# A two-layer hybrid encoder on one core: attention's values by batches of three positions, and FFN inner tiles in two chunks of 11

## The reference

```python
for i in range(DEPTH):
    h_res = h_res + 0.5 * swiglu(rms_norm(h_res, ffn1_norm[i]), ffn1_w_in[i], ffn1_w_out[i])
    h = rms_norm(h_res, mix_norm[i])
    proj = h @ w_in[i]
    y_a = conv_module(proj[..., :o_conv], ...)          # GLU, causal depthwise conv of 31 taps, LayerNorm, swish
    q, k, v = ...                                       # 16 query heads, 4 key/value heads of 64, RMS-normed q and k
    y_b = window_sink_attention(q, k, v, attn_sinks[i]) @ attn_w_out[i]
    merged = gates[..., :D_MODEL] * y_a + gates[..., D_MODEL:] * y_b
    h_res = h_res + merged @ w_out[i]
    h_res = h_res + 0.5 * swiglu(rms_norm(h_res, ffn2_norm[i]), ffn2_w_in[i], ffn2_w_out[i])
```

## Time and profile before

| | us |
|---|---|
| runs | 2418.34, 2423.99, 2425.91 (median 2423.99) |
| profiled execution, its own time | 2424.94 |
| its span | 2423.1 |
| PE busy | 2378.2 (98%), 17637 instructions |
| DVE busy | 1720.2 (71%) |
| ACT busy | 1222.0 (50%) |
| POOL busy | 345.3 (14%) |
| granted TensorE clock, mean | 0.992 |

### The profile page before, as it was taken

One profiled execution on the slowest core, in us unless ns is written; L12 is line 12 of the kernel. 1 busy time (PEld: TensorE's weight loads), 2 busy tenths in 40 slices (PEclk: granted clock), 3 DMA queues, 4 the chain that ended last, 5 costly groups with the idle time before them and its releaser, 6 DMA issues.

```text
span 2423.1 us, 43031 instructions
## 1 busy us (share of the span) xinstructions
PE 2378.2 (98%) x17637; PEld 2236.9 (92%) x17637; DVE 1720.2 (71%) x2740; ACT 1222.0 (50%) x1991; POOL 345.3 (14%) x454
## 2 busy tenths in 40 slices
PE   7999999999999999999999999999999999999999
PEld 6999999999999999999989999998888777889897
DVE  8766664798886477667787676647888855867584
ACT  7554543443444375546565455543434454746371
POOL 1010101121112210101001101011211122101010
PEclk9999999999999999999999999999999999999999
DMA  6655646666667966556546556466676698657472
GB/s 172 154 136 147 154 111 140 145 146 144 139 141 172 209 134 152 145 144 155 146 106 161 141 145 151 112 146 145 145 153 144 130 217 191 144 143 175 116 176 92
DMA packets 106756, 358.69 MB, mean 148 GB/s; under 512 B 12096, under 2 KB 12096, under 8 KB 106560
## 3 DMA queue, kind: packets, MB, share of 16 engines
q0 software_dynamic: 64080, 210.53, 43.0%
q1 hardware_dynamic: 42112, 145.08, 19.8%
q10 hardware_dynamic: 368, 0.33, 0.0%
HBM read 351.41 MB, written 2.10 MB: 146 GB/s over the span
## 4 chain that ended last, share of the span: by engine, by line
PE 87%; DVE 4%; DMA 4%; ACT 3%; issue 2%; POOL 0%; DVEq 0%; ACTq 0%; SPq 0%
PE po L1061 30%; PE po L1078 20%; PE po L1127 19%; PE ptr L1078 8%; PE pov L1078 5%; DMA wla<-in_mixes 1%; PE pov L1289 1%; PE pov L1287 1%; PE ptr L1268 1%; PE pstat L1252 1%; DMA raw<-in_pairs 1%; PE pov L1224 1%; DVE rms L1520 0%; PE pstat L1227 0%; DMA wha<-in_mixes 0%
## 5 line engine op out<-in xcount | busy, mean ns | idle before, releaser
L1061 PE MATMUL po<-xh,wha 128*128 128x264 f32 (+1 forms) x1408 | 348.2, 314 | 4.5 <-DMA wla<-in_mixes 3.9
L1061 PE MATMUL po<-xl,wha 128*128 128x264 f32 (+1 forms) x1408 | 339.2, 308 | 0.0
L1061 PE MATMUL po<-xh,wla 128*128 128x264 f32 (+1 forms) x1408 | 338.4, 307 | 0.0
L1670 DVE SCALAR_TENSOR_TENSOR cv<-ub,lp,cv 128x528 f32<-128x528 f32 (+1 forms) x480 | 333.3, 754 | 1.7
L1061 PEld LDWEIGHTS po<-xh,wha 128*128 128x128 f32 x1408 | 230.3, 191 | 23.3 <-DVE t L1873 3.5
L1078 PE MATMUL po<-x7h,wha 128*128 128x264 f32 (+1 forms) x844 | 241.1, 286 | 4.1 <-ACT tmp L702 1.6
L1078 PE MATMUL po<-x7l,wha 128*128 128x264 f32 (+1 forms) x844 | 240.3, 285 | 0.0
L1061 PEld LDWEIGHTS po<-xh,wla 128*128 128x128 f32 x1408 | 229.7, 191 | 11.3
L1078 PE MATMUL po<-x7h,wla 128*128 128x264 f32 (+1 forms) x844 | 239.8, 284 | 0.0
L1061 PEld LDWEIGHTS po<-xl,wha 128*128 128x128 f32 x1408 | 229.7, 191 | 10.3
L658 ACT ACTIVATE wla<-wha 128x1024 fp32r<-128x1024 f32 x136 | 143.1, 1054 | 162.2 <-DMA wha<-in_mixes 162.1
(11 more groups left out here) (247 smaller groups left out, 6297.0 us busy)
## 6 DMA issues: line engine op xcount, KB each, us to landing
wha<-in_mixes POOLq DMA_DIRECT2D x136, 512.0 KB, 4.4
wla<-in_mixes POOLq DMA_DIRECT2D x136, 512.0 KB, 6.4
raw<-in_pairs SPq DMA_DIRECT2D x88, 768.0 KB, 5.1
wlb<-in_pairs POOLq DMA_DIRECT2D x45, 512.0 KB, 7.6
raw<-in_pairs SPq DMA_DIRECT2D x88, 256.0 KB, 5.9
wla<-in_pairs POOLq DMA_DIRECT2D x87, 256.0 KB, 6.7
wfa<-in_outs SPq DMA_DIRECT2D x48, 448.0 KB, 3.4
wla<-in_pairs POOLq DMA_DIRECT2D x41, 512.0 KB, 8.2
```

The costliest lines, as they stand in the source:

```text
L1061: ins = mm(po[:, 2 * out_slot + h, 0:width], w[:, k, :], v[:, k, t:t + width], start=begin and k == 0 and p == 0, stop=last and k == kt - ...
L1670: stt(cv[:, j, a:], u, w, cv[:, j, a:], ALU.mult, ALU.add).then_inc(conv_step, 1)
```

## The change

1. The attention's values are made for the three positions of a batch at once. `turn` and `take_pt` of single positions become, for a batch, `turn_later` (the windows of its second and third position, four transposes, which fill the bank `ptr`), `take_windows`, `turn_first` (the first position's windows and one transpose of all meta probabilities of the batch), `take_metas` and `mix_values`.
2. To have one transpose of the meta probabilities, `norm_p` writes them to a tile of their own, `pm` (96 columns), in an instruction of its own, and the windows in another; it waits for the meta transpose of the batch before.
3. The meta product of a position is two products, one for each half of the array's columns, with 96 rows: the weights `vz` are zero in the rows of the other positions. `head_stats` makes the meta values three times, at the partitions of the three positions, by six products with the identity, and `head_std` copies six pieces.
4. The steps stand at other places among the blocks of `mixer_in` and `attn_out_start`, and in ACT's order.
5. The inner tiles of an FFN run in two chunks of 11. A row of output products has two blocks of weights, of 6 and of 5 k-tiles, so that a chunk has 16 blocks (`NB`) for 8 rows. The ring of three remains, its buffers in another order. `out_hi` and `out_lo` serve two blocks a row.
6. `hh` and `hl` hold 11 tiles for 8, and the memory set aside for POOL's transfers is set to 4096 (`dynamic_dma_scratch_size`).

```diff
-CHUNKS = ((0, 7), (7, 14), (14, KF))
+CHUNKS = ((0, 11), (11, KF))
+CHUNK_T = 11
+
+BLOCKS = ((0, 6), (6, CHUNK_T))
+NB = KD * len(BLOCKS)
...
-OUT_UNITS = ((0, 2, 4), (8, 10, 12))
+OUT_UNITS = ((2, 4, 0), (10, 12, 8))
...
-    return USED["out", s, c, {"A": 6, "S12": 7, "S43": 5}[part]]
+    return USED["out", s, c, {"A": NB - 2, "S12": NB - 1, "S43": NB - 3}[part]]
...
-    return USED[("P2", "P6", "P7")[m], s * KF + CHUNKS[c][1] - 2]
+    return USED[("P6", "P7", "P2")[m], s * KF + CHUNKS[c][1] - 2]
...
-    return USED["out", 2 * l, len(CHUNKS) - 1, n + 4]
+    return USED["out", 2 * l, len(CHUNKS) - 1, NB - 4 + n]
...
                     for m in range(KD):
                         if m:
-                            out_hi(s, c, m + 2)
+                            out_hi(s, c, 2 * m + 2)
+                        out_hi(s, c, 2 * m + 3)
...
-            def take_pt(l, g, pos):
...
+            def take_windows(l, g, b):
+
+                act.wait_ge(tr_ready, 2 * batch(l, g, b) + 1)
+                act.wait_ge(pv_done, batch(l, g, b) + 1)
+                func(pt[:, 1:, :, :], ptr[:, :].rearrange("p (i h n) -> p i h n", i=2, h=2), ACT.Copy)\
+                    .then_inc(pt_ready, 1)
+
+            def take_metas(l, g, b):
+
+                act.wait_ge(tr_ready, 2 * batch(l, g, b) + 2)
+                if b:
+                    func(pt[:, 0, :, :], ptr[:, 0:2 * P].rearrange("p (h n) -> p h n", h=2), ACT.Copy)
+                n = MR - metas_from(l, b) * MB
+                func(ptm[0:n, :], ptr[0:n, 2 * P:3 * P], ACT.Copy).then_inc(pt_ready, 1)
...
-                    take_pt(l, g, 0)
+                    take_windows(l, g, 0)
                     fill_tanh(l, g, 7)
-                    attn_exp(l, g, 1, 0)
-                    take_pt(l, g, 1)
-                    attn_exp(l, g, 1, 1)
-                    attn_exp(l, g, 1, 2)
+                    for i in range(SB):
+                        attn_exp(l, g, 1, i)
                     h(8)
-                    take_pt(l, g, 2)
+                    take_metas(l, g, 0)
...
-                tr(pov[0:META, 64:64 + HD], kvp[HD:P, PAD:PAD + META], ident[HD:P, HD:P])
-                tr(pov[0:MB, 128:128 + HD], kvp[HD:P, PAD + META - MB:PAD + META], ident[HD:P, HD:P])\
-                    .then_inc(qk_stat, 1)
+                for c, t in ((64, PAD), (128, PAD + META - MB)):
+                    for i in range(SB):
+                        ins = mm(pov[i * MB:(i + 1) * MB, c:c + HD], kvp[HD:P, t:t + MB], ident[HD:P, HD:P], start=True,
+                                 stop=True)
+                ins.then_inc(qk_stat, 1)
...
+            def mix_values(l, g, b):
+
+                pe.wait_ge(pt_ready, 2 * batch(l, g, b) + 3)
+                pe.wait_ge(o_lo, batch(l, g, b) + 1)
...
+                    if pos:
+                        for h in range(2):
+                            mm(dst[h * HD:(h + 1) * HD], vw[:, pos - 1, :], cut(pt[:, i, h, :]), start=True,
+                               stop=False, skip_group_check=True)
                     for h in range(2):
-                        mm(dst[h * HD:(h + 1) * HD], vw[:, pos - 1, :], cut(pt[:, h, :]), start=True,
-                           stop=False, skip_group_check=True)
-                mm(dst, vm[:, :], cut(ptm[:, :]), start=pos == 0, stop=True,
-                   skip_group_check=True).then_inc(pv_done, 1)
+                        ins = mm(dst[h * HD:(h + 1) * HD], vz[0:n, i - i0, h, :], cut(ptm[0:n, :]), start=pos == 0,
+                                 stop=True, skip_group_check=True)
+                ins.then_inc(pv_done, 1)
...
-                    mids = {7: do(lambda: S(1)), 8: do(lambda: V(0), lambda: T(1)),
-                            9: do(lambda: V(2), lambda: T(3)), 10: do(lambda: V(4), lambda: T(5))}
-                    ends = {3: do(lambda: head_stats(l, g)), 5: do(lambda: S(0)), 7: do(lambda: T(0)),
-                            8: do(lambda: V(1), lambda: T(2), lambda: S(2)),
-                            9: do(lambda: V(3), lambda: T(4)), 10: do(lambda: V(5), lambda: T(6))}
+                    mids = {7: do(lambda: S(1)), 8: do(lambda: F(0)), 9: do(lambda: L(1)), 10: do(lambda: V(1))}
+                    ends = {3: do(lambda: head_stats(l, g)), 5: do(lambda: S(0)), 7: do(lambda: L(0)),
+                            8: do(lambda: V(0), lambda: S(2)), 9: do(lambda: F(1)), 10: do(lambda: L(2))}
...
-                            out_lo(s, c, m + 2)
+                            out_lo(s, c, 2 * m + 2)
+                        out_lo(s, c, 2 * m + 3)
...
+                dve.wait_ge(tr_ready, 2 * batch(l, g, b))
+                tt(pm[:, :].rearrange("p (i h k) -> p i h k", i=SB, h=2)[:, i0:, :, :],
+                   w[:, i0:, WIN:WIN + MB].rearrange("p i (h k) -> p i h k", h=2),
+                   rd.to_broadcast([P, SB - i0, 2, META]), ALU.mult)
...
-    nc = bacc.Bacc("TRN2", target_bir_lowering=False, num_devices=1)
+    nc = bacc.Bacc("TRN2", target_bir_lowering=False, num_devices=1, dynamic_dma_scratch_size=4096)
```

More of the change, by code:

```diff
@@ L502, in lead, with batch, metas_from @@
             return 1 if l == LAST else 0
-        def place(l, g, pos):
-            if l == LAST:
-                return l * GROUPS * NPOS + g * (NPOS - 1) + pos - 1
-            return (l * GROUPS + g) * NPOS + pos
+        def batch(l, g, b):
+            return (l * GROUPS + g) * NBAT + b
+        def metas_from(l, b):
+            return max(lead(l) - b * SB, 0)
         def o_from(l, b):
@@ L895, in take_o @@
             def take_o(l, g, b):
-                act.wait_ge(pv_done, place(l, g, (b + 1) * SB) + 1)
+                act.wait_ge(pv_done, batch(l, g, b) + 2)
                 dst, src = o_view(ah[:, 2 * g:2 * g + 2, :], l, b)
@@ L1255, in scores, with turn_windows @@
                 ins.then_inc(s_ready, 1)
-            def turn(l, g, pos):
-                if pos < lead(l):
-                    return
-                n = place(l, g, pos)
-                b, i = pos // SB, pos % SB
-                pe.wait_ge(p_ready, (l * GROUPS + g) * NBAT + b + 1)
-                pe.wait_ge(pt_ready, n + 1)
-                if pos:
+            def turn_windows(l, g, b, positions):
+                for n, i in enumerate(positions):
                     for h in range(2):
@@ L1901, in laid_out @@
             for a, b in CHUNKS:
-                outs += [block(f"{name}_w_out", l, a, b - a, ((m * P, P),)) for m in range(KD)]
+                for m in range(KD):
+                    outs += [block(f"{name}_w_out", l, a + k, z - k, ((m * P, P),)) for k, z in BLOCKS]
         for n in range(NBLK):
```

177 lines of the change are left out of this document (89 added, 88 removed).

## The result

| | us |
|---|---|
| runs after | 2387.31, 2391.09, 2391.75, 2393.29 (median 2391.42) |
| runs before, same chip | median of four 2421.68 (2418.34 to 2425.91) |
| ratio | 0.9868, 95% interval 0.9851 to 0.9885 |
| profiled execution after, its span | 2391.75, 2390.0 |
| granted TensorE clock, mean | 0.990 |

The change made the kernel 1.3% faster, 30.3 us by the medians on one chip, 33.2 by the two profiled executions (2424.94 to 2391.75). The forecast was 2407 with a range down to 2394: right in sign, half the size (17 us of 30 to 33), and outside its range by 2.6 us.

What follows compares the result with a forecast made beforehand. TensorE, busy 98% of the span, was taken as the bound. From 2424.94 us profiled, -17.2 + 3.3 + 1.4 - 3.1 - 2.1 - 1.3 + 2 = -17.0 gave 2407.9, stated as 2407 for the median; range 2394 to 2422.

Steps and rivals of the forecast that it cites:

- the transposes: Attention insertions of each batch: later windows' transposes at 0.73 us, the first position's with the meta transpose at 0.48.
- chunk ends: FFN: eight ends losing 0.43 us each, where twelve lost 6.6 us in all: -3.1 us.
- chunk starts: FFN: uneven pairs after inner chunk starts lose 4.3 us with their drains; half remains: -2.1 us.
- late base weights: FFN: the base weights of a chunk's second pair arrive 0 to 1 us late a start: +2 us for four.
- values of three: Attention: six pairs of half-width products, the first at 0.38 us, followers at 0.275, plus 0.1: 1.86 us a batch.
- set-up's products: Each group's values set-up: six f32 products replace two small transposes, 0.4 us net a group: +3.3 us in eight groups.
- wait for the meta copy: First batch's values at block 8's end wait for ACT's meta copy, 0.9 us in the second group: +1.4 us in all.
- end of layer 0's second FFN: Longer rows let DVE keep up, returning 2.3 us, less 1 for late splits after rows 1, 3 and 5: -1.3 us.
- rival 2: Attention: the meta copy is late in all eight groups by 1 to 2 us: +10, 2417 at worst; chance 0.12.
- (1): Attention values: halves do not overlap, a pair costs 0.38 us, 11.3 us less gain: 2418; chance 0.17.
- (3): FFN output blocks' ring: release to split passes 8.04 us, slowing each block; at 9 us +38, 2445; chance 0.06.
- (4): Descriptor memory of 4096 makes POOL wait before issuing the mixer's 136 blocks: up to +122, 2529; chance 0.03.

Runs made afterwards that it cites:

- e15: The kernel before with only its set-up cut into three stretches: ratio 0.9965, median 2414.5 us.
- e13: The changed kernel with the set-up in three stretches, at the ends of blocks 2, 3 and 4: ratio 0.9819, median 2378.6 us.
- e1: The kernel before with only the descriptor memory set to 4096: ratio 1.0003, median 2425.0 us.
- e9: The changed kernel run once more, unchanged: ratio to the kernel before 0.9858, median 2391.3 us.
- e4: The FFN part with descriptor memory, but three chunks of 7, 7 and 8 tiles and halved output blocks, attention as before: ratio 1.0064, median 2441.9 us.
- e5: The changed kernel with all 96 rows kept in the meta products of layer 1's first batches, for 64: ratio 0.9843, median 2388.2 us.
- e12: Second run of the changed kernel with two small transposes for the six products of the meta keys' values: ratio 0.9862, median 2390.3 us.
- e2: The kernel before with the attention part and descriptor memory, FFN as before: ratio 0.9919, median 2405.3 us.
- e10: The changed kernel with VectorE splitting three k-tiles once more ahead of the split of a chunk's second output block: ratio 0.9881, median 2396.5 us.
- two-stretch kernel: The changed kernel with the set-up divided, sums of squares at block 3's end, values' transposes and six products at block 4's: ratio 0.9814, median 2381.4 us.

## Why the prediction was wrong

Two steps failed. The larger is a term of the sum that was mis-sized, the transposes: 0.73 and 0.48 us an insertion were forecast, 0.35 and 0.25 measured, and with them the attention gave 29.0 us where 17.2 stood in the sum. The other is the FFN's terms, of which chunk ends (-3.1, measured -5.7), chunk starts (-2.1, measured -4.0) and late base weights (+2, measured 0) were carried over, halved or allowed for without reading what ends each loss. The clock was at no step, and its loss at the set-ups hid some of both errors.

Measured insertion costs below are the time between two projection products with the attention's step between them, less 0.122 us for the product itself; -33.2 us is to be explained.

| step | forecast | measured |
|---|---|---|
| one position, before | 1.28 | 1.19 |
| later windows | 0.73 | 0.35 |
| first position and meta | 0.48 | 0.25 |
| values of three | 1.86 | 1.63 |
| attention, eight groups | -17.2 | -29.0 |
| set-up's products | +3.3 | +1.9 |
| wait for the meta copy | +1.4 | +3.05 (second execution 1.80) |
| clock at the set-up | none | +7.2 (means of two executions each: +4.9) |
| late weights (3.9 to 1.7 us) and other waits, mixer | none | -2.4 |
| chunk ends | -3.1 | -5.7 |
| chunk starts | -2.1 | -4.0 |
| base weights late | +2 | 0 |
| end of layer 0's second FFN, at full clock | -1.3 | +1.3 |
| clock at that end | none | -3.3 |
| pace of output products | 0 | -2.0 |
| clock in the first 52 us | none | -2.6 |
| clock in the last FFN | none | +1.4 |

**Attention: right mechanism, wrong size.** A group of layer 0 went from 10.17 us to 6.14 (forecast 10.9 to 8.65), in layer 1 from 9.65 to 6.44: 4 x 4.03 + 4 x 3.21 = 29.0. The pair was nearly right (0.233; the six of a batch are 0.23 us below). The transposes were not: I charged 0.37 for two and 0.1 for entering, from the earlier trace rows, where they stand behind the 32-row meta product. Two at 0.22 and four at 0.44 is their own price, and the two at 1659.12 in the trace before had it. The prediction had the meta product's change of form in hand and applied it to the values alone. Of the 1.8 us a group between forecast and result the transposes are 1.8, the values 0.8, and the position before, which was 0.09 cheaper by the same ruler, takes 0.75 back.

**Set-up.** Full clock against full clock (e15, e13) the step costs 1.09 for 0.85 us: 0.24 x 8, near the low bound of 0.2. **Meta copy.** The place, its cause and the size of one wait were right; the group was not: none in layer 0's second group, one in its fourth, two in layer 1, where rival 2 was held to be least likely; three groups of eight and not all.

**The clock** was no step at all. The page's mean of 0.992 was read as full. Behind the two transposes of the earlier trace rows it stood at 0.50 from 417 to 420 us, and the prediction read no clock there. Late weights (the -2.4) are no sure gain either: the changed kernel's second execution has 3.3 us of them.

**FFN.** Four terms were wrong and all in one direction. For the chunk ends I took over today's smallest loss (0.43) without asking what ends it: it is a split of 7 or 8 k-tiles on DVE, and the change makes blocks of 5 and 6. Seven of eight ends lose nothing beyond the change itself. The second pair of a chunk came in time, with no wait for base weights: 0.2 us to spare by medians was enough. Past chunk starts the losses went from 4.35 to 0.37 us; "half remains" had no row behind it. In the output products 4200 matmuls went from 0.12175 to 0.12128 us each; there are 32 starts of a row fewer, which may be why.

The end of layer 0's second FFN did not do what was said. 2.3 us of waiting were to come back and 1 to be paid. PE's waits there for an eviction, a bank and the rebuilt operand went from 3.3 us (0.48, 0.53 and 2.29) to 1.7 (1.2 and 0.5), so 1.6 came back, and waits on the split after rows 1, 3 and 5 cost 1.43, 0.31 and 0.20. With the small losses beside them this end costs 1.3 us more at full clock, not 1.3 less. It is shorter all the same, 5.8 us of losses for 7.8, because 3.3 of the 7.8 were products at half pace while the clock stood at 0.50 behind the wait of 2.29 (the row at 1240 above). e1's execution fell there too, and e9's, like the one after, did not.

The first 52 us of the execution before had a stretch at half clock (45.9 to 51.6) that another execution of the same program (e1) didn't have; this 2.6 us isn't the change's. Nor is the fall that the last FFN has after the change (at 2067.2) and not before, +1.4. The terms give -19.3 and -14.9; the stages -19.3 and -14.0.

**The range.** Its low end let the pair, the set-up, the copy and the base weights come out well, which is 12.0 us below 2407 (2395, where 2394 is written). The transposes, the chunk ends and the chunk starts had no low case, and there the time was.

**The rivals.** (1) is out: 0.23, not 0.38. (2) happened at a third of its price. (3) wasn't reached at 8.04 us of cover except behind the rebuild of the operands (the three split waits above); with half blocks e4 shows it. (4) is out by e1.

## What to carry to other kernels

Ask of every small stall which instruction ends it, and whether the change resizes that instruction: one gain here was a VectorE split that became 0.3 us shorter. Take the price of an instruction from a place where its neighbours are like those it will have; beside another tile shape it carries the change of shape. Where PE's work is cut into a stream of tiny products, spread them among the large ones, and read the granted clock in windows of a few microseconds rather than its mean. Do the same before a shorter stretch is put down to a wait: at the end of layer 0's second FFN the clock gave back more than the waits did.

## What the hardware showed that was not expected

- The granted clock fell to 0.5 in or behind stretches of small products: set-ups of 3.6 to 4.0 us (2 to 8 groups of eight, differently in executions of one program) and of 2.8 to 3.0 us (3 and 6); never behind the stretches of 1.1 to 1.9 us of the three kernels with the cut set-up. It stayed down for some 3 to 7 us, 1.1 to 2.7 us lost each time.
- It fell behind plain waits of PE as well, and there a length alone doesn't decide. After a meta copy's wait of 1.93 us (e13) and one of 2.44 (e5, at 1875.6) it fell, after one of 2.01 (e12, at 1871.0) it did not; behind 2.29 to 2.31 us at the end of layer 0's second FFN it fell in all four executions of kernels with the FFN as before. A wait of some 1.75 us for ACT early in the last FFN had a fall behind it in the execution after, in e2, e10 and e12, and none in the execution before, in e1 or in e9, which is the changed kernel again.
- The Trainium skill, TensorE: Matmul & The Clock Gate, Part 1, tells of a kernel's start that the observation of PE's activity runs freely and that the number of slow matmuls differs from run to run. Falls in the middle of this kernel agree: eight and five in two executions of one program.
- A pair of half-width products costs 0.23 us behind its like and 0.37 behind one of another number of rows, whether 64 or 32; 96 rows are like 128.
- What stays open: which stretches a fall follows and which not, so also why the two-stretch kernel had three falls after its set-ups and the same with three more edits six. Each count is one profiled execution.
